# First head unit starts with tokens 0 to 255; weight lows all on VectorE

## The reference

```python
h = rms_norm(x, attn_norm[0])                # [512, 1024]
q, k, v = split(h @ a_w_in)                  # 16 q heads, 4 k heads, 4 v heads of 64
q, k = partial_rope(q), partial_rope(k)
p = softmax(q k^T over this chunk and the one before, and a sink)
x = x + (p v) @ a_w_out
x = x + conv_ffn(rms_norm(x, ffn_norm[0]))
```

## Time and profile before

| | us |
|---|---|
| median of 3 runs | 1210.06 (1209.37 to 1210.58) |
| profiled execution | 1208.92 |
| its span | 1207.1 |
| TensorE busy | 1164.9 (97%) |
| VectorE busy | 712.0 (59%) |
| ScalarE busy | 475.1 (39%) |
| GpSimd busy | 18.8 (2%) |

### The profile page before, as it was taken

One profiled execution on the slowest core, in us unless ns is written; L12 is line 12 of the kernel. 1 busy time (PEld: TensorE's weight loads), 2 busy tenths in 40 slices (PEclk: granted clock), 3 DMA queues, 4 the chain that ended last, 5 costly groups with the idle time before them and its releaser, 6 DMA issues.

```text
span 1207.1 us, 16143 instructions
## 1 busy us (share of the span) xinstructions
PE 1164.9 (97%) x5820; PEld 980.6 (81%) x5820; DVE 712.0 (59%) x1152; ACT 475.1 (39%) x929; POOL 18.8 (2%) x36
## 2 busy tenths in 40 slices
PE   6999899999999999999999999989999999999996
PEld 6988778888888878887888888768888888878885
DVE  5577867556655563335667777765665556553335
ACT  6565645312222223334655555644222212222325
POOL 4100000000000000000000000000000000000000
PEclk9999999999999999999999999999999999999998
DMA  7311203332333312324312221114233333322231
GB/s 209 79 36 36 70 1 107 104 95 80 103 104 104 87 37 103 104 88 138 106 53 53 53 73 49 36 41 134 81 94 104 104 91 83 87 70 98 93 103 71
DMA packets 146476, 101.44 MB, mean 84 GB/s; under 512 B 12065, under 2 KB 139270, under 8 KB 146438
## 3 DMA queue, kind: packets, MB, share of 16 engines
q1 hardware_dynamic: 146438, 100.93, 28.6%
HBM read 98.82 MB, written 2.10 MB: 84 GB/s over the span
## 4 chain that ended last, share of the span: by engine, by line
PE 81%; DVE 11%; ACT 6%; issue 1%; DMA 1%; SPq 0%; DVEq 0%; ACTq 0%
PE ps L499 21%; PE ps L501 21%; PE ps L500 21%; PE ps L564 11%; PE ps L578 2%; DVE w_lo L1282 2%; ACT w_hi L964 1%; PE ps L716 1%; ACT prob L1037 1%; DVE den L1373 1%; ACT prob L1028 1%; PE ps L633 1%; DVE h_lo L1311 1%; DVE den L1355 1%; DMA raw<-in_a_w_in 1%
## 5 line engine op out<-in xcount | busy, mean ns | idle before, releaser
L964 ACT ACTIVATE w_hi<-raw 128x512 fp32r<-128x512 f32 (+2 forms) x212 | 192.8, 941 | 301.5 <-PE ps L501 300.6
L499 PE MATMUL ps<-h_hi,w_lo 128*128 128x512 f32 x704 | 274.7, 390 | 0.0
L501 PE MATMUL ps<-h_hi,w_hi 128*128 128x512 f32 x704 | 273.9, 389 | 0.0
L500 PE MATMUL ps<-h_lo,w_hi 128*128 128x512 f32 x704 | 273.9, 389 | 0.0
L1282 DVE TENSOR_TENSOR w_lo<-raw,w_hi 128x512 fp32r<-128x512 f32 (+2 forms) x204 | 215.7, 1082 | 6.2 <-ACT w_hi L964 6.2
L499 PEld LDWEIGHTS ps<-h_hi,w_lo 128*128 128x128 f32 x704 | 132.2, 188 | 28.0 <-issue 0.5
L500 PEld LDWEIGHTS ps<-h_lo,w_hi 128*128 128x128 f32 x704 | 132.2, 188 | 28.0 <-issue 0.5
L501 PEld LDWEIGHTS ps<-h_hi,w_hi 128*128 128x128 f32 x704 | 132.2, 188 | 27.1
L564 PE MATMUL ps<-w_hi,h_lo 128*128 128x384 f32 x384 | 133.5, 348 | 13.9 <-DVE w_lo L1282 6.4
L499 PE MATMUL ps<-u_hi,w_lo 128*128 128x512 f32 x352 | 137.3, 390 | 1.1 <-DVE u_all L1576 0.6
L501 PE MATMUL ps<-u_hi,w_hi 128*128 128x512 f32 x352 | 137.0, 389 | 0.0
(11 more groups left out here) (170 smaller groups left out, 1488.4 us busy)
## 6 DMA issues: line engine op xcount, KB each, us to landing
raw<-in_ffn_w_up SPq DMA_DIRECT2D x88, 512.0 KB, 4.6
raw<-in_ffn_w_down SPq DMA_DIRECT2D x44, 512.0 KB, 3.3
raw<-in_b_w_in SPq DMA_DIRECT2D x24, 512.0 KB, 5.3
raw<-in_a_w_out SPq DMA_DIRECT2D x4, 1024.0 KB, 5.0
raw<-in_b_w_out SPq DMA_DIRECT2D x4, 1024.0 KB, 5.0
raw<-in_a_w_in SPq DMA_DIRECT2D x3, 1024.0 KB, 7.0
x_tok<-in_x SPq DMA_DIRECT2D x4, 512.0 KB, 5.1
out<-x_tok SPq DMA_DIRECT2D x8, 256.0 KB, 2.9
```

Of the source, the lines that this page charges most:

```text
L499: pe.matmul(out_, a_lo, b_hi, start=start, stop=False)
L500: pe.matmul(out_, a_hi, b_lo, start=False, stop=False)
L501: return pe.matmul(out_, a_hi, b_hi, start=False, stop=stop)
L964: act.activation(w_hi[:, s, at], raw[:, s, at], ACT.Copy).then_inc(hi_done, 1)
```

## The change

Unit 0's front is done in two pairs of token tiles. Transfers: x tiles 0 and 1, unit 0's weights, x tiles 2 and 3, unit 1's weights. TensorE transposes only tiles 0 and 1 first, two slabs to a PSUM bank (banks 4 to 7), then `first_pair` does their products slab by slab, and behind the products of slabs 3 to 6 (`FIRST_BACK`) it transposes two slabs of tiles 2 and 3. The products of tiles 2 and 3 are sorted by slab too. ScalarE makes h_hi in halves of 256 tokens (`gained0`), with unit 0's w_hi parts between; the squares of tiles 1 to 3 and the norm's factor come after the first pair's h_hi; unit 1's first two w_hi parts come before `take` of tile 2, the others before that of tile 3. VectorE copies and makes h_lo in halves, with unit 0's w_lo parts between. GpSimd's loop of lows is gone: unit 1's w_lo parts 0 and 1 stand behind low_v of tiles 2 and 3, parts 2 and 3 behind the rotation.

```diff
@@ SP
-            for t in range(NT):
+            for t in range(2):
                 sp.dma_start(x_tok[:, t, :], xv[:, t, :]).then_inc(x_landed[t], 16)
...
             load_attn("attnA", 0, 0, slice(KC // 2, KC), raw_landed[0])
+            for t in range(2, NT):
+                sp.dma_start(x_tok[:, t, :], xv[:, t, :]).then_inc(x_landed[t], 16)
@@ GpSimd
-            for i in range(FIRST_LOWS):
-                low("attnA", i, i)
@@ TensorE
+            def first_pair():
...
+                for kc in range(KC):
+                    if kc % 2 == 0:
+                        pe.wait_ge(lo_done, part_done("attnA", 0, kc // 2))
+                    pe.wait_ge(hlo_done0, kc + 1)
+                    for t in range(2):
+                        tok = slice(t * P, (t + 1) * P)
+                        ins = hi_lo(ps[:, t, 0:UW], h_hi[:, kc, tok], h_lo[:, kc, tok],
+                                    wh[:, kc, :], wl[:, kc, :], start=(kc == 0), stop=(kc == KC - 1))
...
+                    if kc >= FIRST_BACK:
+                        for t in range(2, NT):
+                            pe.wait_ge(x_landed[t], 16)
+                        for k in (2 * (kc - FIRST_BACK), 2 * (kc - FIRST_BACK) + 1):
...
+                            pe.wait_ge(x_ready0, k // 2 * 2 + 2)
+                            for t in range(2, NT):
+                                ins = pe.transpose(first_x(k, t), x_tok[:, t, k * P:(k + 1) * P], ident[:, :])
+                            ins.then_inc(x_tr, 1)
@@ ScalarE
             square_tokens(0)
-            square_tokens(1)
             for kc in range(KC):
-                gained(NORM["A"], kc, vecT[:, 0, R_ATTN + kc:R_ATTN + kc + 1])
...
-            square_tokens(2)
-            square_tokens(3)
+                gained0(0, kc)
+                if kc % 2 == 0:
+                    high0(kc // 2)
+            for t in range(1, NT):
+                square_tokens(t)
...
             rsqrt(NORM["A"], rstd_tok[:, :], x_ss[:, :], 1.0 / D)
-            high("attnA", 1, 0, None, 0)
-            for t in range(NT):
+            for kc in range(KC):
+                gained0(1, kc)
+                if kc % 4 == 3:
+                    take("A", 0, 0, kc // 4)
+            for t in range(2, NT):
+                high("attnA", 1, 0, None, 2 * (t - 2))
+                high("attnA", 1, 0, None, 2 * (t - 2) + 1, wait=False)
                 take("A", 0, 0, t)
@@ VectorE
-            for kc in range(KC + 2):
...
+            copy_x(0, 0)
+            copy_x(0, 1)
+            for kc in range(KC):
+                if kc % 2 == 0:
+                    low_w("attnA", 0, 0, kc // 2)
+                low_h0(0, kc)
+                if kc + 2 < KC:
+                    copy_x(0, kc + 2)
+            copy_x(1, 0)
+            copy_x(1, 1)
+            for kc in range(KC):
+                low_h0(1, kc)
+                if kc + 2 < KC:
+                    copy_x(1, kc + 2)
@@ VectorE, first_scores
                 for t in range(NT):
                     low_v(kind, 0, 0, t)
+                    if kind == "A" and t >= 2:
+                        low_w("attnA", 1, 1, t - 2)
...
                 rope(kind, 0)
                 if kind == "A":
+                    for c in range(2, 4):
+                        low_w("attnA", 1, 1, c)
                     little_vectors()
```

More of the change, by code:

```diff
@@ L44 @@
 UA, UB = 4, 8
+FIRST_BACK = 3
 OB, ODC = 4, 2
@@ L66 @@
 CONSTS = 1 + HALF + 4 + 10
-FIRST_LOWS = 2
 ALU = mybir.AluOpType
@@ L270, in trunk, with first_x, pair_cols @@
         dve_self = sem("dve_self")
+        def first_x(kc, t=None):
+            if t is None:
+                return ps[:, 4 + kc // 2, (kc % 2) * 2 * P:(kc % 2 + 1) * 2 * P]
+            return ps[:, 4 + kc // 2, (kc % 2 * 2 + t % 2) * P:(kc % 2 * 2 + t % 2 + 1) * P]
+        def pair_cols(pair):
+            return slice(pair * 2 * P, (pair + 1) * 2 * P)
         def qk_bank(u, c):
@@ L550, in projection @@
                 order = [(t, kc) for t in tiles for kc in range(KC)]
-                if coming and first_unit:
+                if first_unit and (coming or kind == "A"):
                     order.sort(key=lambda x: x[1])
@@ L570, in projection @@
                             yield
+            def first_pair():
+                wh = w_hi[:, 0, :].rearrange("p (k n) -> p k n", k=KC)
+                wl = w_lo[:, 0, :].rearrange("p (k n) -> p k n", k=KC)
+                pe.wait_ge(posT_done, 2)
+                for kc in range(KC):
+                    if kc % 2 == 0:
+                        pe.wait_ge(lo_done, part_done("attnA", 0, kc // 2))
+                    pe.wait_ge(hlo_done0, kc + 1)
+                    for t in range(2):
+                        tok = slice(t * P, (t + 1) * P)
+                        ins = hi_lo(ps[:, t, 0:UW], h_hi[:, kc, tok], h_lo[:, kc, tok],
+                                    wh[:, kc, :], wl[:, kc, :], start=(kc == 0), stop=(kc == KC - 1))
+                        if kc == KC - 1:
+                            ins.then_inc(proj_done, 1)
+                    if kc >= FIRST_BACK:
+                        for t in range(2, NT):
+                            pe.wait_ge(x_landed[t], 16)
+                        for k in (2 * (kc - FIRST_BACK), 2 * (kc - FIRST_BACK) + 1):
+                            if k >= KC:
+                                continue
+                            pe.wait_ge(x_ready0, k // 2 * 2 + 2)
+                            for t in range(2, NT):
+                                ins = pe.transpose(first_x(k, t), x_tok[:, t, k * P:(k + 1) * P], ident[:, :])
+                            ins.then_inc(x_tr, 1)
             def run(slabs, k):
@@ L592, in start_unit0 @@
             def start_unit0(kind):
-                slabs = chain(projection(kind, 0, 0, (0, 1)), projection(kind, 0, 0, (2, 3)))
-                run(slabs, 12 + 8)
+                if kind == "A":
+                    first_pair()
+                    slabs = projection(kind, 0, 0, (2, 3))
+                    run(slabs, 8)
+                else:
+                    slabs = chain(projection(kind, 0, 0, (0, 1)), projection(kind, 0, 0, (2, 3)))
+                    run(slabs, 12 + 8)
                 if kind == "B":
@@ L1056, in square_tokens, with gained0, high0 @@
                                accum_out=x_ss[:, t:t + 1]).then_inc(x_sq, 1)
+            def gained0(pair, kc):
+                act.wait_ge(x_ready if pair else x_ready0, kc + 1)
+                at = pair_cols(pair)
+                act.activation(h_hi[:, kc, at], xT[:, kc, at], ACT.Copy,
+                               scale=vecT[:, 0, R_ATTN + kc:R_ATTN + kc + 1])\
+                   .then_inc(hhi_done if pair else hhi_done0, 1)
+            def high0(c):
+                if c == 0:
+                    act.wait_ge(half_landed, 16 * 3)
+                high("attnA", 0, 0, None, c, wait=(c == 2))
             square_tokens(0)
-            square_tokens(1)
             for kc in range(KC):
-                gained(NORM["A"], kc, vecT[:, 0, R_ATTN + kc:R_ATTN + kc + 1])
[L1062 to L1065, removed]
-            square_tokens(2)
-            square_tokens(3)
+                gained0(0, kc)
[3 more added lines that the diff above has]
+                square_tokens(t)
             act.wait_ge(const_done, CONSTS)
@@ L1412, in _, with copy_x, low_h0 @@
             dve.wait_ge(posT_tr, 2)
-            dve.tensor_copy(vecT[:, 0, R_ATTN:R_ATTN + KC], ps[:, 6, 0:KC]).then_inc(posT_done, 1)
+            dve.tensor_copy(vecT[:, 0, R_ATTN:R_ATTN + KC], ps[:, 1, 0:KC]).then_inc(posT_done, 1)
             dve.wait_ge(posT_done, 2)
-            for kc in range(KC + 2):
[L1416 to L1420, removed]
+            def copy_x(pair, kc):
+                dve.wait_ge(x_tr if pair else x_tr0, kc // 2 * 2 + 2)
+                dve.tensor_copy(xT[:, kc, pair_cols(pair)], first_x(kc)).then_inc(x_ready if pair else x_ready0, 1)
+            def low_h0(pair, kc):
+                dve.wait_ge(hhi_done if pair else hhi_done0, kc + 1)
+                at = pair_cols(pair)
+                dve.scalar_tensor_tensor(out=h_lo[:, kc, at], in0=xT[:, kc, at],
+                                         scalar=vecT[:, 0, R_ATTN + kc:R_ATTN + kc + 1],
+                                         in1=h_hi[:, kc, at].bitcast(F32), op0=ALU.mult,
+                                         op1=ALU.subtract).then_inc(hlo_done if pair else hlo_done0, 1)
+            copy_x(0, 0)
[12 more added lines that the diff above has]
+                    copy_x(1, kc + 2)
             def little_vectors():
```

25 lines of the change are left out of this document (11 added, 14 removed).

## The result

| us | before | after |
|---|---|---|
| median of 20 runs | 1210.61 (1208.16 to 1211.52) | 1212.97 (1211.13 to 1214.28) |
| profiled execution | 1208.92 | 1214.28 |
| its span | 1207.1 | 1212.5 |
| second pair begins | 27.15 | 25.09 |
| unit 1 begins | 35.47 | 35.59 |

The changed kernel is slower: ratio 1.0025, 95% interval 1.0019 to 1.0031, by medians 2.4 us. The prediction was 1212.4, 2.3 over before. The last three rows are instants of the two profiled executions, in us from the start of the span: the first product of tiles 2 and 3, the first of unit 1, and the first transposes of q and k (fill_qk). The executions of one kernel differ among themselves: of the 73 of the kernel before that were taken beside the experiments, nearly all with a mean granted clock of 0.994 or more measured 1208.1 to 1209.8, and nearly all at 0.993 or less 1209.7 to 1211.7.

A forecast was written before the change was run, and what follows sets the result against it. TensorE carries most of the span, so only its waits, in the first 45 us, could be gained. -2.35 +1.9 +1.25 +1.3 +0.2 made +2.3 us, on a median of 1210.06 giving 1212.4; range 1209.2 to 1215.4.

The forecast's parts named there:

- Part 1, transfers: With x tiles 2 and 3 behind unit 0's weights, half of those weights lands at 9.5 instead of 12.48.
- Part 2, lows on VectorE: A low costs 0.95 on VectorE against 2.14 on GpSimd, and about 1.0 us per h_lo goes as well.
- Part 3, the round: In the first pair, two slabs form one closed round through VectorE and ScalarE of 2.98 us.
- Part 4, the second pair: Second pair waits for three ScalarE squares and starts at 24.8 against 27.15, a gain of 2.35 us.
- Part 5, the new waits: TensorE waits 1.9, 1.25 and 1.3 us for VectorE's unit 1 lows; fill_qk at 42.1 to 42.2 against 39.88.
- The sum: Up to fill_qk: -2.35 for the earlier pair, +1.9, +1.25, +1.3 for waits, +0.2 for restarts: +2.3 us.
- faster rival: Unit 1's lows are off TensorE's path, the earlier second pair reaches the end: -2.35, 1207.7; chance 0.08.
- tighter round: First pair's round is only VectorE's own time, 2.33: -0.6 to +1.5, 1209.5 to 1211.6; chance 0.20.
- The clock: Clock falls in the sparse stretch before fill_qk, slabs 4 to 7 at 0.32: +1.8, in all 1214.2; chance 0.12.
- The row that spoke for a full clock: Profile stage 573.4 to 577.4, which kept full clock with TensorE busy 2.17 of 4.00 us; by it the sum holds.
- the line at 0.2%: About 2.4 us, what a measurement of this kernel can tell from no change; slower 0.49, same 0.43, faster 0.08.

The follow-up runs named there:

- e8: Changed kernel with SP again issuing all four tiles of x ahead of unit 0's weights: 1215.42, ratio to before 1.0053.
- b1: Kernel before with unit 0's four w_lo parts moved from GpSimd to VectorE: 1209.15, ratio to before 0.9996.
- e6: Changed kernel with all eight w_lo parts of units 0 and 1 back on GpSimd, pairs kept: 1211.50, ratio to before 1.0010.
- e7: Changed kernel with four useless matmuls between TensorE's first transposes and first products: 1213.30, ratio to before 1.0031.
- e4: Changed kernel with ScalarE's squares of tiles 1 to 3 inside the first pair's rounds: 1213.07, ratio to before 1.0028.
- e1: Changed kernel with all unit 1 w_hi parts before ScalarE's take of tile 2, all w_lo before VectorE's low_v of tile 2: 1208.24, ratio to before 0.9983.
- e2: Changed kernel with unit 1's four w_lo parts back on GpSimd, unit 0's staying on VectorE: 1210.36, ratio to before 1.0009.
- e9: Changed kernel with four useless matmuls in TensorE's hole between the second pair and unit 1: 1212.91, ratio to before 1.0029.
- e3: Changed kernel with the second pair's products run tile after tile instead of slab by slab: 1213.08, ratio to before 1.0024.
- f2: Changed kernel with early unit 1 lows, squares inside rounds, first-pair copies first and four useless matmuls before the first products: 1205.13, ratio to before 0.9967.

## Why the prediction was right, step by step

- **Part 1, transfers:** said 9.5, measured 9.62 in this profile, w_hi between 9.13 and 10.99 in eleven profiles with this order. e8 shows the term.
- **Part 2, lows on VectorE:** the price of each instruction was right (0.96 and no long h_lo). The prediction lets it look like a gain; b1 and e6 show it as next to none.
- **Part 3, the round:** said 2.98, measured 3.00.
- **Part 4, the second pair:** said 24.8, measured 25.09, and 15.45 to 15.47 after the landing in seven profiles (15.3 by my terms). The squares are the cause by e7 (a faster TensorE moves nothing) and e4 (without them 1.1 us). One thing was missed: the half clock lasted until 17.8, 16 matmul distances and not one round of 12, so TensorE itself was only 0.24 us from being the bound in this profile and 1.1 in e4's.
- **Part 5, the new waits:** the step that decides. Said unit 1 at 35.1, part 1 at 37.4, part 2 at 39.9, fill_qk at 42.2; measured 35.6, 37.8, 40.3, 43.1. e1 takes the order away and 4.7 us with it, e2 takes the engine and part of the order away and gets 2.6 (5.1 and 1.9 by the ratios).
- **The sum** in measured terms: -2.06 for the second pair's start, +2.18 to unit 1's start, +3.09 from there to fill_qk, +3.21; said -2.35, +2.0, +2.65. The extra 0.44 of the last term is the clock by e9, where the same stretch is 0.56 shorter. The lower end of the range, 1209.2, has no working in the prediction: its faster rival gives 1207.7 and its tighter round starts at 1209.5. The +1.5 at the upper side of the tighter round isn't worked out either.
- **The clock** had 0.12 and a price of 1.8 us. It fell in all five profiles that have the sparse stretch unfilled and unit 1's lows behind tiles 2 and 3 (changed, e3, e4, e7, e8) and not in e9, which fills part of it. The chance was too small. The price of 1.8 was near the 1.4 and 1.6 of e8 and e7, where most matmuls of slabs 4 to 7 ran at 0.32, and too high for the changed kernel's profile, where only the first few of them did and it was 0.56. The row that spoke for a full clock, 2.17 us busy of 4.00, was one draw: that very stage lost its clock in five of fourteen profiles.
- The page "TensorE: Matmul & The Clock Gate" of the Trainium skill, section "HAM oscillation — how this bites in real kernels", warned of gaps between bursts: e9 agrees with it, since filling one gap kept the clock up, though the two later gaps stayed. That a VectorE instruction with two SBUF inputs contends with a GpSimd instruction that reads SBUF ("SBUF — State Buffer", section "Who interferes with whom", of the Trainium skill) is borne out by e2 (0.35 to 1.98 for a two-input instruction) and e6 (0.47 to 1.81).
- Forecast and time: 1212.4 against 1212.97. The slower side of the line at 0.2% was given 0.49 and happened, by 0.05%; the interval's lower end, 0.19%, is not clear of the line. That 2.3 and 2.4 agree to 0.1 us is in part luck. The mechanism is the one that was worked out, step by step, but at fill_qk the profile is 3.2 us behind and not 2.3 or 2.4, and one profile can't say how the landing (which varies by 1.9 us) and the falls of the clock are spread over the twenty runs.

## What to carry to other kernels

An earlier start is worth what the next stage can take: here 2 us of lead ended at work that VectorE was to do behind it and that GpSimd had done under cover. When work moves from an idle engine to a strictly ordered queue, look at what stands in front of it there, and put it ahead of anything that waits for the stage that it must be ready for. Moving unit 1's lows up by a few lines turned a loss of 0.25% into a gain of 0.17%.

## What was not expected of the hardware

- The first products ran at the 1.2 GHz spacing (0.32 us) for 5.8 us after an idle time of 3.3 us, while the record of the granted clock says 1.00 for that stretch. The spacing of starts is the surer witness. With four useless matmuls in the idle time (e7, f2) no matmul of the first pair was at that spacing.
- With the same transfers in the same order, the first half of the weights landed between 9.1 and 11.0 us in eleven profiles. Every later instant of the front moved with it by the full amount, so profiles of this kernel are to be compared from that landing on.
- The same stage of the second layer, with TensorE waiting 1.83 to 1.86 us for h_lo, kept the full clock in the kernel before and lost it in five of fourteen profiles (changed, e1, e4, e6, e9). A single trace in which the clock held is weak evidence that it will hold.
- Two inputs from SBUF beside a GpSimd subtraction: 0.35 became 1.98 us for 192 columns, 0.47 became 1.70 to 1.81 for 256, and 0.74 became 1.65 to 1.86 for 512. The shortest instruction loses most and all end up about as long as one of GpSimd's subtractions (1.8 to 2.1 us). That fits a wait for the other engine's instruction better than a share of the instruction's own length; no run here separates the two further.
